# Latent attention of the decode tokens, four sequences at a time in 32-column tiles of TensorE

## The chip, the cores and the metric

The kernel runs on one NeuronCore of a Trainium2 chip, written instruction by instruction with semaphores. The engines are TensorE (PE; its weight loads are listed apart as PEld), VectorE (DVE), ScalarE (ACT), GpSimd (POOL) and SyncE (SP), which issues most DMAs. The metric is the device time of one execution in microseconds. The kernel before took 2738.17, 2734.61 and 2735.32 us in three runs: median 2735.32. TensorE has two clock levels, 1.2 and 2.4 GHz; a granted clock of 1.00 in the profile is the higher one.

## The reference

One layer of a decoder step for 1024 prompt tokens and 8 sampled tokens (8 sequences, one new token each, 2048 cached positions). The change is in the latent attention of the 8 sampled tokens:

```python
def mla_sample(q_nope, q_rope, latent_new, past_latent, w_uk, w_uv):
    scale = (MLA_NOPE_DIM + MLA_ROPE_DIM) ** -0.5          # 64 + 32
    q_abs = jnp.einsum('bthd,chd->bthc', q_nope, w_uk)     # 8 heads, 128 latent dims
    def scores(lat):
        s = (jnp.einsum('bthc,bkc->bhtk', q_abs, lat[..., :MLA_KV_RANK])
             + jnp.einsum('bthr,bkr->bhtk', q_rope, lat[..., MLA_KV_RANK:]))
        return s.astype(jnp.float32) * scale
    ...
    p = jax.nn.softmax(jnp.concatenate([scores(past_latent), s_new], axis=-1), axis=-1)
    o_lat = (jnp.einsum('bhtk,bkc->bthc', p[..., :past_len], past_latent[..., :MLA_KV_RANK])
             + jnp.einsum('bhtk,bkc->bthc', p[..., past_len:], latent_new[..., :MLA_KV_RANK]))
    return jnp.einsum('bthc,chd->bthd', o_lat, w_uv)
```

`past_latent` is gathered from a paged cache: 16 pages of 128 rows for each sequence, 160 values a row (128 latent, 32 rotary). All arrays are fp32.

## The kernel before

The program goes through feed-forward 1, the input projections, the prompt's latent attention (16 steps for each of 4 head pairs), then the **decode latent stage**, then the dilated window attention (prompt and decode together), the merge, and feed-forward 2. The order on each engine is the order of the code; semaphores connect them. Large products are written as three matmuls on fp32r operands: an operand is split into `hi` (rounded) and `lo` (the rest).

The decode latent stage (PE lines 1067 to 1133, ACT 1598 to 1621, DVE 1926 to 1981, POOL 744) works so:

- SP loads the pages of sequence pairs one by one into `latn` (line 563, one issue for each page, with the page number read into a register). The last loads are issued while the stage runs.
- POOL copies the 32 rotary values of each cached row three times side by side into `kr_nat`, 1536 columns for a sequence.
- For each of 32 units (sequence b, four pages) PE transposes 4 pages of latents (L1078) and 4 of rotary values (L1079) into PSUM banks 4 + u%2 and 6 + u%2. ACT copies them to `lt_hi` and `krm` (L1610, L1611), DVE writes the rests `lt_lo` and the middle third of `krm` (L1949, L1951).
- PE then multiplies with `z_hi`, `z_lo`, `z_rope` (L1101 to L1104, four matmuls of 512 columns): zero-padded query blocks, which put the 8 heads of each sequence in their own 8 of 64 rows, so that all eight sequences accumulate in PSUM banks 0 to 3. The transposes of unit u+2 are issued before the scores of unit u.
- One softmax for 64 rows by 2048 columns (DVE maximum L1958, ACT exponential L1613, DVE scale L1970), 16 transposes of the probabilities (L1110), copies by ACT.
- Values (L1121, L1123): for each sequence 1 + 16 plain fp32 matmuls, with 8 columns of probabilities as the weights and 128 latent columns moving. Then transposes, `w_uv` (L1132), and the store into `om_hi`, `om_lo`.

SP waits for `latn_read` before it loads the window caches `kv_d` into the place of the latents; POOL's and DVE's first dilated steps wait for them. In the code before, the last `latn_read` comes with the last value matmul.

Of the kernel before, what the change touches and what calls it, by code (L numbers as in the profile page):

```python
# [20 lines left out]
F32 = mybir.dt.float32  # L21
# [8 lines left out]
P = 128  # L30
# [71 lines left out]
def build(nc, io):  # L102
    with ExitStack() as ctx:
# [13 lines left out]
        seq_mask = sb("seq_mask", [NS * MH, NS])  # L117
# [78 lines left out]
        lt_hi = at(24576, "lt_hi", [P, 4, 512], F32R)  # L196
        lt_lo = at(32768, "lt_lo", [P, 4, 512], F32R)
        krm = at(40960, "krm", [96, 4, 512], F32R)
        kr_nat = at(49152, "kr_nat", [P, 2, NPG, 96])

        z_hi = at(61440, "z_hi", [P, NS * 136], F32R)
        z_lo = at(65792, "z_lo", [P, NS * 136], F32R)
        z_rope = at(70144, "z_rope", [96, NS * 136], F32R)
        wukT = at(74496, "wukT", [64, MH * P])
        wuv = at(78592, "wuv", [P, MH * 64])
        qabs = at(80640, "qabs", [P, NS, MH])
        q_rope = at(80896, "q_rope", [32, NS, MH])
        s_tmp = at(81152, "s_tmp", [NS * MH, NS])
        s_stat = at(81184, "s_stat", [NS * MH, 8])
        s_new = at(81216, "s_new", [NS * MH, NS])  # L210
        s_newT = at(81248, "s_newT", [NS, NS * MH])
        ckv_nat = at(81504, "ckv_nat", [NS, P])
        olat = at(82016, "olat", [P, NS, MH])
        dprobs = at(24576, "dprobs", [NS * MH, PAST])
        dprobsT = at(32768, "dprobsT", [P, NPG, NS * MH])
        olatT = at(36864, "olatT", [MH, NS * P])
# [108 lines left out]
        lt_hi_done = sem("lt_hi_done")  # L325
        lt_lo_done = sem("lt_lo_done")
        lat_read = sem("lat_read")
        latn_read = sem("latn_read")
        q_zeroed = sem("q_zeroed")
        dm_pe = sem("dm_pe")  # L330
        dm_v = sem("dm_v")
        dm_act = sem("dm_act")
# [139 lines left out]
        def pv_ends(S):  # L472
            _, k, kbs = filler(S)
            return k if k is not None and kbs[-1] == 2 * (k % 4) + 1 else None

# [194 lines left out]
        def _(pool):  # L670
# [68 lines left out]
            for b in range(NS):  # L739
                if b % 2 == 0:  # L740
                    pool.wait_ge(latn_landed[b // 2], 16 * 2 * NPG)
                if b >= 2:
                    pool.wait_ge(lt_ready, 4 * (b - 1))
                nc.gpsimd.tensor_tensor(kr_nat[:, b % 2].rearrange("p n (c f) -> p n c f", c=3),
                                        latn[:, latent_slot(b) * NPG:(latent_slot(b) + 1) * NPG, P:LAT].unsqueeze(2).to_broadcast([P, NPG, 3, 32]),
                                        zero[:].unsqueeze(2).unsqueeze(3).to_broadcast([P, NPG, 3, 32]), ALU.add
                                        ).then_inc(kr_packed, 1)
# [15 lines left out]
        def _(pe):  # L763
# [302 lines left out]
            dm = Tally(dm_pe)  # L1066
            def latents_T(u):

                b, k = divmod(u, 4)
                if k == 0 and b % 2 == 0:  # L1070
                    pe.wait_ge(latn_landed[b // 2], 16 * 2 * NPG)
                if k == 0:
                    pe.wait_ge(kr_packed, b + 1)
                if u >= 2:
                    pe.wait_ge(lt_lo_done, 2 * (u - 1))
                for j in range(4):
                    page = 4 * k + j
                    nc.tensor.transpose(ps[:, 4 + u % 2, j * P:(j + 1) * P], latn[:, latent_slot(b) * NPG + page, 0:P], ident[:])  # L1078
                    last = nc.tensor.transpose(ps[0:96, 6 + u % 2, j * P:(j + 1) * P], kr_nat[:, b % 2, page], ident[:])  # L1079
                last.then_inc(lt_ready, 1)  # L1080
# [4 lines left out]

# [6 lines left out]
            pe.wait_ge(dm_v, 4)  # L1092
            pe.wait_ge(dm_act, 4)
            for u in range(4 * NS):
                b, k = divmod(u, 4)
                if u + 2 < 4 * NS:
                    latents_T(u + 2)
                pe.wait_ge(lt_lo_done, 2 * u + 2)
                z = slice(b * P, (b + 1) * P)
                out = ps[:, k, :]  # L1100
# [5 lines left out]
            mm(ps[0:64, 4, 0:NS], qabs[:].rearrange("p b h -> p (b h)"), ckv_s[:], start=True, stop=False)  # L1106
            dm.by(mm(ps[0:64, 4, 0:NS], q_rope[:].rearrange("p b h -> p (b h)"), kr_s[:], start=False, stop=True))
            pe.wait_ge(dm_v, 13)
            for j in range(NPG):
                last = nc.tensor.transpose(ps[:, 5 + j // 8, (j % 8) * 64:(j % 8 + 1) * 64],  # L1110
                                           dprobs[:, j * P:(j + 1) * P], ident[0:64, 0:64])
            dm.by(last)
            nc.tensor.transpose(ps[0:NS, 7, 0:64], s_new[:], ident[0:64, 0:64])
            dm.by(nc.tensor.transpose(ps[0:NS, 7, 64:64 + P], ckv_s[:], ident[:]))
# [1225 lines left out]
```

## Time and profile before

| | |
|---|---|
| median of three runs | 2735.32 us |
| profiled execution | 2738.68 us |
| its span | 2736.6 us, granted clock 0.964 |
| PE busy | 2572.9 us, 94% of the span |
| DVE, ACT, POOL busy | 1100.4, 533.4, 925.0 us |
| decode latent stage, from the last prompt-attention store to the first dilated scores | 1493.9 to 1615.5 us |

A program with PE busy in 94% of its span is bound by PE nearly everywhere, but not in this stage alone: there the busy share, the clock and the engine that ends a wait change from stretch to stretch. The page's totals do not tell this; the table of stretches and the chain of waits below do. A matmul's duration in the profile includes the way through the array, so the pace is read from start to start, or from a merged row of many.

### The profile page before, as it was taken

Reading aid. Unit: us, or ns where it says so; the run is one execution under the profiler, and the core shown is the slowest. Engines: PE = TensorE matmul, PEld = TensorE weight load, DVE = VectorE, ACT = ScalarE, POOL = GpSimd, SP = SyncE. Lnnn points to the kernel's source line nnn. Section 1 sums busy time; section 2 is a strip of 40 time slices with the busy share of each in tenths; the row PEclk is TensorE's granted clock in tenths of the full one; section 3 lists DMA queues with packets and bytes.
Section 4 is the critical chain, followed back from the end, with each engine's and each line's share of the span. In section 5 each row is a group of like instructions: output and inputs, shape, how many; then the busy total and the mean of one; then the engine's idle time right before and its main releaser. Section 6 shows DMA issues by size and latency. Waiting matters only on the chain.

```text
span 2736.6 us, 40136 instructions
## 1 busy us (share of the span) xinstructions
PE 2572.9 (94%) x15962; PEld 2426.5 (89%) x15962; DVE 1100.4 (40%) x1881; ACT 533.4 (19%) x1250; POOL 925.0 (34%) x468
## 2 busy tenths in 40 slices
PE   4999999999989999999888889889899999999996
PEld 4999999999979998998555758789799999999996
DVE  7122222222274663101667624473612222222226
ACT  4100000000022430213334513211310000000002
POOL 5333333333354340531000210234333333333332
PEclk9999999999999999999999987789899999999998
DMA  4121212121222341421202142463112211111111
GB/s 157 68 90 68 90 68 89 68 89 68 89 99 91 136 144 46 142 91 61 66 14 69 58 157 101 139 204 117 41 64 82 95 47 47 47 47 47 47 47 62
DMA packets 85101, 229.38 MB, mean 84 GB/s; under 512 B 8681, under 2 KB 47122, under 8 KB 83826
## 3 DMA queue, kind: packets, MB, share of 16 engines
q1 hardware_dynamic: 78858, 207.86, 22.0%
q10 hardware_dynamic: 6088, 19.23, 1.8%
q8 instruction: 126, 2.06, 0.3%
q14 instruction: 29, 0.24, 0.0%
HBM read 196.65 MB, written 74.39 MB: 99 GB/s over the span
## 4 chain that ended last, share of the span: by engine, by line
PE 51%; DVE 5%; issue 2%; ACT 2%; DMA 2%; POOL 0%; SPq 0%; DVEq 0%; ACTq 0%; POOLq 0%
PE ps L768 13%; PE ps L769 12%; PE ps L770 12%; PE ps L1219 1%; PE ps L1034 1%; PE ps L1016 1%; PE ps L1123 1%; PE ps L881 1%; PE ps L883 1%; PE ps L882 1%; DMA sgt<-scratch_gates 1%; PE ps L1001 1%; PE ps L1184 1%; PE ps L1202 1%; PE ps L1078 1%
## 5 line engine op out<-in xcount | busy, mean ns | idle before, releaser
L768 PE MATMUL ps<-u_hi,w_hi 128*128 128x352 f32 (+1 forms) x2880 | 933.1, 324 | 25.3 <-DVE u_lo L403 18.9
L769 PE MATMUL ps<-u_lo,w_hi 128*128 128x352 f32 (+1 forms) x2880 | 925.2, 321 | 0.0
L770 PE MATMUL ps<-u_hi,w_lo 128*128 128x352 f32 (+1 forms) x2880 | 923.2, 321 | 0.0
L677 POOL TENSOR_TENSOR w_hi<-raw,zero 128x1024 fp32r<-128x1024 f32 x184 | 352.6, 1916 | 1322.3 <-PE ps L768 1108.3
L768 PEld LDWEIGHTS ps<-u_hi,w_hi 128*128 128x128 f32 x2880 | 545.8, 189 | 36.1 <-DVE u_lo L403 17.6
L769 PEld LDWEIGHTS ps<-u_lo,w_hi 128*128 128x128 f32 x2880 | 546.5, 190 | 0.5 <-issue 0.3
L770 PEld LDWEIGHTS ps<-u_hi,w_lo 128*128 128x128 f32 x2880 | 545.6, 189 | 0.0
L680 POOL TENSOR_TENSOR w_lo<-raw,w_hi 128x1024 fp32r<-128x1024 f32 x184 | 450.4, 2448 | 14.4
L1735 DVE TENSOR_TENSOR h<-ps,silu 128x352 f32<-128x352 f32 x132 | 68.2, 516 | 750.6 <-PE ps L770 745.3
L1744 DVE SCALAR_TENSOR_TENSOR x<-ps,x 128x352 f32<-128x352 f32 (+1 forms) x528 | 270.9, 515 | 211.8 <-PE ps L770 211.6
L768 PE MATMUL ps<-h_hi,w_hi 128*128 128x352 f32 (+1 forms) x1056 | 344.0, 326 | 10.0 <-DVE x L1744 7.3
L769 PE MATMUL ps<-h_lo,w_hi 128*128 128x352 f32 (+1 forms) x1056 | 340.9, 323 | 0.0
L770 PE MATMUL ps<-h_hi,w_lo 128*128 128x352 f32 (+1 forms) x1056 | 340.0, 322 | 0.0
L768 PEld LDWEIGHTS ps<-h_hi,w_hi 128*128 128x128 f32 x1056 | 200.5, 190 | 18.7 <-DVE x L1744 18.3
L1387 ACT ACTIVATE silu<-ps 128x352 f32<-128x352 f32 x132 | 60.7, 460 | 757.5 <-PE ps L770 757.5
L769 PEld LDWEIGHTS ps<-h_lo,w_hi 128*128 128x128 f32 x1056 | 200.8, 190 | 0.3
L770 PEld LDWEIGHTS ps<-h_hi,w_lo 128*128 128x128 f32 x1056 | 201.1, 190 | 0.0
L1391 ACT ACTIVATE h_hi<-h 128x352 fp32r<-128x352 f32 x132 | 65.2, 494 | 494.7 <-DVE h L1735 494.7
L1739 DVE TENSOR_TENSOR h_lo<-h,h_hi 128x352 fp32r<-128x352 f32 x132 | 101.8, 771 | 65.0 <-ACT h_hi L1391 65.0
L1436 ACT ACTIVATE swapped<-ps 32x352 f32<-32x352 f32 (+1 forms) x144 | 64.9, 450 | 87.2 <-PE ps L770 74.6
L1320 ACT ACTIVATE sq<-x 128x352 f32<-128x352 f32 (+1 forms) x96 | 45.4, 489 | 158.4 <-DVE x L1744 80.2
L1001 PE MATMUL ps<-kT,qT 128*128 128x512 f32 (+3 forms) x192 | 74.0, 495 | 2.1 <-ACT probs L1545 2.1
(271 smaller groups left out, 2767.0 us busy)
## 6 DMA issues: line engine op xcount, KB each, us to landing
raw<-in_wstream SPq DMA_DIRECT2D x186, 512.0 KB, 3.2
out_win_out<-in_cache_win SPq DMA_DIRECT2D x23, 1424.0 KB
latn<-in_cache_mla SPq DMA_DIRECT2D x128, 80.0 KB, 1.9
scratch_gates<-stage ACTq DMA_DIRECT2D x16, 516.0 KB, 2.6
out_win_out<-in_cache_win SPq DMA_DIRECT2D x7, 1168.0 KB
kv_d<-in_cache_win SPq DMA_DIRECT2D x24, 256.0 KB, 9.0
sgt<-scratch_gates SPq DMA_DIRECT2D x16, 352.0 KB, 4.1
scratch_x_mid<-x SPq DMA_DIRECT2D x1, 4128.0 KB, 13.3
```

The source lines that it names most:

```text
L677: nc.gpsimd.tensor_tensor(hi, raw[:, s % RAW], zero[:].to_broadcast([P, UW]), ALU.add).then_inc(w_hi_done, 1)
L680: nc.gpsimd.tensor_tensor(lo, raw[:, s % RAW], hi.bitcast(F32), ALU.subtract).then_inc(split_done, 1)
L768: a = mm(out, wh, xh, start=start, stop=False)
L769: mm(out, wh, xl, start=False, stop=False)
L770: return a, mm(out, wl, xh, start=False, stop=stop)
L1001: last = mm(ps[:, bank, 0:w], qT[i % 2][h][:, n * P:(n + 1) * P], kT[i % 2][h][:, a * P:a * P + w], start=True, stop=not diag)
L1387: A(silu[:, b, 0:w], ps[:, t, 0:w], ACT.Silu).then_inc(silu_done, 1)
L1391: A(h_hi[:, par, c, tile(t)], h32[:, b, 0:w], ACT.Copy).then_inc(h_hi_done, 1)
L1436: last = A(swapped[a:a + 32, e % 2, 0:w], ps[b:b + 32, bank, 0:w], ACT.Copy)
L1735: V.tensor_tensor(h32[:, b, 0:w], ps[:, 3 + t, 0:w], silu[:, b, 0:w], ALU.mult).then_inc(h_mul, 1)
L1739: V.tensor_tensor(h_lo[:, par, c, tile(t)], h32[:, b, 0:w], h_hi[:, par, c, tile(t)].bitcast(F32), ALU.subtract).then_inc(h_ready, 1)
L1744: V.scalar_tensor_tensor(x[:, m, tile(t)], ps[:, 6 + j % 2, 0:TILES[t][1]], 0.5, x[:, m, tile(t)], ALU.mult, ALU.add).then_inc(down_evac, 1)
```

## The change

- The split of latents and queries is dropped in the scores: plain fp32 matmuls, which the profile records as two instructions each.
- Four sequences form a group; two groups r = 0, 1. In a group, sequence q has the 32 columns 32q to 32q+31 of the array (8 heads used, the rest zero), so its scores fall into PSUM partitions 32q to 32q+31. The weights are `qabs[:, b]` (128 by 32), the moving operand `lt` (128 by 512).
- Rotary part: POOL packs 16 pages by 32 values without repeats; one transpose turns four pages into a 128 by 128 block `krT`; the weights `q_rope[:, i]` hold the query in rows 32i to 32i+31 and zeros elsewhere, so four matmuls of 128 columns do the four pages.
- PSUM units are copied once, by ACT and DVE in turns.
- Each group has its own softmax over 128 rows by 2048 columns. The normalization moves behind the values. PE does the transposes of later units meanwhile.
- Values: four matmuls next to each other with 128 by 32 weights and `latn` moving; `latn_read` is raised by 4 after each group.

```diff
+            def decode_scores(quad):
+                r, k = divmod(quad, 4)
+                pe.wait_ge(lt_act, 4 * quad + 4)
+                pe.wait_ge(lt_dve, 4 * quad + 4)
...
+                if quad == 4:
+                    pe.wait_ge(dm_act, DMA_EXP[0])
+                for q in range(4):
+                    mm(ps[32 * q:32 * q + 32, k, :], qabs[:, 4 * r + q], lt[:, (4 * quad + q) % 8],
+                       start=True, stop=False, skip_group_check=True)
+                for i in range(4):
+                    for q in range(4):
+                        last = mm(ps[32 * q:32 * q + 32, k, i * P:(i + 1) * P], q_rope[:, i, 4 * r + q],
+                                  krT[:, (4 * quad + q) % 8], start=False, stop=i == 3, skip_group_check=True)
+                last.then_inc(dsc_ready, 1)
...
-                mm(out, z_hi[:, z], lt_hi[:, u % 4], start=b == 0, stop=False)
-                mm(out, z_lo[:, z], lt_hi[:, u % 4], start=False, stop=False)
-                mm(out, z_hi[:, z], lt_lo[:, u % 4], start=False, stop=False)
-                mm(out, z_rope[:, z], krm[:, u % 4], start=False, stop=b == NS - 1).then_inc(lat_read, 1)
...
+                            last = mm(ps[rows, bank, 0:P], dprobsT[:, r, j, rows],
+                                      latn[:, latent_slot(4 * r + q) * NPG + j, 0:P], start=False, stop=j == NPG - 1,
+                                      skip_group_check=True)
+                last.then_inc(latn_read, NS // 2)
...
+            for u in range(2, 8):
+                latents_T(u)
...
+            for quad in range(8):
+                decode_scores(quad)
+                if quad < 6:
+                    for q in range(4):
+                        latents_T(4 * (quad + 2) + q)
+            decode_PT(0)
+            decode_values(0)
+            decode_PT(1)
+            decode_values(1)
...
+            def latents_copy(u):
+                act.wait_ge(lt_ready, u + 1)
...
+                if u % 2:
+                    A(lt[:, u % 8], ps[:, 4 + u % 2, :], ACT.Copy).then_inc(lt_act, 1)
+                else:
+                    A(krT[:, u % 8], ps[:, 6 + u % 2, 0:P], ACT.Copy).then_inc(lt_act, 1)
...
+            for u in range(20):
+                latents_copy(u)
+            decode_exp(0)
+            for u in range(20, 32):
+                latents_copy(u)
```

On PE, the end of one unit of the score loop before: the last of four pairs of transposes of unit u+2 (`latn`, `kr_nat`), then the four split matmuls of unit u, which accumulate over all sequences.

```order
L1078 MATMUL ps<-ident,latn_99 128x128
L1079 MATMUL ps<-ident,kr_nat_103 96x128
L1101 MATMUL ps<-lt_hi_100,z_hi_104 128x512
L1102 MATMUL ps<-lt_hi_100,z_lo_105 128x512
L1103 MATMUL ps<-lt_lo_101,z_hi_104 128x512
L1104 MATMUL ps<-krm_102,z_rope_106 128x512
```

The same place now: the end of the new-token scores, the first quad of scores and the transposes of unit 8, which those of units 9 to 11 follow.

```order
L1162 MATMUL ps<-ckv_s,qabs_105 128x8
L1164 MATMUL ps<-kr_s,q_rope_106 128x8
L1099 MATMUL ps<-lt_100,qabs_105 32x512 x4
L1103 MATMUL ps<-krT_101,q_rope_106 32x128 x16
L1082 MATMUL ps<-ident,latn_99 128x128 x4
L1083 MATMUL ps<-ident,kr_nat_103 128x128
```

A quad of scores is 20 matmuls on 32-row outputs, between blocks of four units of transposes (5 each, not 8); the new-token scores moved from behind the loop to ahead of it.

On PE behind the scores, now: `dprobs` are the probabilities, `s_new` and `ckv_s` the new token's.

```order
L1099 MATMUL ps<-lt,qabs 32x512 x4
L1103 MATMUL ps<-krT,q_rope 32x128 x16
L1118 MATMUL ps<-ident,dprobs 128x128 x16
L1124 MATMUL ps<-ident,s_new 8x128
L1126 MATMUL ps<-ident,ckv_s 8x128
L1140 MATMUL ps<-ckv_nat,s_newT 32x128 x4
L1143 MATMUL ps<-latn,dprobsT 32x128 x64
```

This block of transposes and values comes once for each group, where before 16 transposes stood ahead of all eight sequences' values.

On DVE, where the first softmax stands among the copies (the end of unit 19 and the start of unit 20 around it):

```order
L2011 COPY krT<-ps 128x128 [waits dsc_ready,lt_ready]
L2017 TENSOR_REDUCE s_stat<-ps 128x1 [waits dsc_ready]
L2020 TENSOR_TENSOR s_stat<-s_stat 128x1 [waits dm_v]
L2022 TENSOR_SCALAR s_stat<-s_stat 128x1 [waits dm_v]
L2013 COPY lt<-ps 128x512 [waits dsc_ready,lt_ready]
```

The maximum over the first group stands ahead of the copies of unit 20; ACT has its exponential at the same place. In the kernel before no softmax step stood among the copies.

## Rows read from the trace of the kernel before

**Rows 1.** From the page: the span, and the page loads (x, KB, us to landing).
```profile
span 2736.6 us, 40136 instructions
latn<-in_cache_mla SPq DMA_DIRECT2D x128, 80.0 KB, 1.9
```

**Rows 2.** Stretches: us, busy (x) of PE, PEld, DVE, ACT, POOL; clock; DMA; GB/s.
```profile
1493.90:1507.50 13.60, 6.03 (x32) 5.56 (x32) 9.64 (x12) 4.22 (x9) 5.75 (x2) 0.62 0.22 60
1507.50:1568.70 61.20, 60.23 (x372) 48.60 (x372) 42.80 (x64) 32.41 (x60) 16.49 (x6) 0.97 0.18 62
1568.70:1579.30 10.60, 2.86 (x20) 1.99 (x20) 4.79 (x10) 3.33 (x5) 0.00 (x0) 0.51 0.00 0
1579.30:1611.90 32.60, 32.58 (x271) 23.73 (x270) 0.00 (x0) 0.00 (x0) 0.00 (x0) 0.95 0.01 2
```

**Rows 3.** Chain that ended last: start us, us, what.
```profile
1332.86 1.72 PE ps L1001 x4
1493.95 3.10 DVE z_hi L1929
1497.04 3.75 DVE z_lo L1929
1501.41 3.56 PE ps L1089 x16
1568.81 2.21 DVE s_stat L1958
1571.41 2.06 ACT dprobs L1613 x2
1584.89 3.59 PE ps L1123 x32
1613.30 5.64 DMA kv_d<-in_cache_win
```

**Rows 4.** Timeline of the loop: start us, us, engine, line, work [idle before].
```profile
1496.04 0.30 PE L1078 MATMUL ps<-ident,latn 128*128 128x128 f32 x1 [2.97 <-POOL kr_nat L744]
1507.83 0.42 PE L1079 MATMUL ps<-ident,kr_nat 128*96 128x128 f32 x1
1509.11 0.42 PE L1079 MATMUL ps<-ident,kr_nat 128*96 128x128 f32 x1
1511.11 0.27 PE L1079 MATMUL ps<-ident,kr_nat 128*96 128x128 f32 x1
1511.76 0.27 PE L1079 MATMUL ps<-ident,kr_nat 128*96 128x128 f32 x1
1563.93 0.27 PE L1079 MATMUL ps<-ident,kr_nat 128*96 128x128 f32 x1
1564.24 0.60 ACT L1610 ACTIVATE lt_hi<-ps 128x512 fp32r<-128x512 f32 x1 [0.73 <-PE ps L1079]
```

**Rows 5.** Groups, 1489.6 to 1615.6: work xcount, busy us, mean ns, idle before.
```profile
L744 POOL TENSOR_TENSOR kr_nat<-latn,zero 128x1536 f32<-128x1536 f32 x8 | 23.0, 2878 | 151.1 <-PE ps L1034 115.2 <-PE ps L1079 35.9
L1949 DVE TENSOR_TENSOR lt_lo<-ps,lt_hi 128x512 fp32r<-128x512 f32 x32 | 22.1, 692 | 15.8 <-ACT krm L1611 15.7
L1610 ACT ACTIVATE lt_hi<-ps 128x512 fp32r<-128x512 f32 x32 | 19.1, 597 | 28.4 <-PE ps L1079 28.4
```

**Rows 6.** Timeline, column tiles of 64 and a switch of tiling.
```profile
1486.98 0.63 PEld L1034 LDWEIGHTS ps<-probsT,v_pair 128*64 128x64 f32 x8 [0.17 <-issue]
1489.61 3.46 PE L1034 MATMUL ps<-probsT,v_pair 128*64 128x256 f32 x32 [0.73 <-DVE probsT L1896]
1614.16 0.64 PE L1132 MATMUL ps<-olat,wuv 128*64 128x8 f32 x16 [0.32 <-DVE olat L1977]
```

**Rows 7.** Stretches, for the granted clock.
```profile
1511.00:1568.00 57.00, 56.39 (x358) 45.34 (x357) 40.93 (x60) 31.33 (x58) 16.49 (x6) 1.00 0.18 63
1497.30:1507.50 10.20, 4.77 (x23) 4.27 (x20) 6.24 (x10) 3.11 (x8) 2.35 (x1) 0.50 0.23 64
```

**Rows 8.** Timeline, SyncE: the last page loads.
```profile
1482.78 32.79 SPq L563 DMA_DIRECT2D latn<-in_cache_mla  x25
```

More of the change, by code:

```diff
@@ L741, in _ @@
                     pool.wait_ge(latn_landed[b // 2], 16 * 2 * NPG)
[L742 to L746, printed above, removed]
+                nc.gpsimd.tensor_tensor(kr_nat[:, b].rearrange("p (n f) -> p n f", f=32),
+                                        latn[:, latent_slot(b) * NPG:(latent_slot(b) + 1) * NPG, P:LAT],
+                                        zero[:].unsqueeze(2).to_broadcast([P, NPG, 32]), ALU.add
                                         ).then_inc(kr_packed, 1)
@@ L1067, in latents_T @@
             def latents_T(u):
-                b, k = divmod(u, 4)
-                if k == 0 and b % 2 == 0:
+                quad, q = divmod(u, 4)
+                r, k = divmod(quad, 4)
+                b = 4 * r + q
+                if k == 0 and q % 2 == 0:
                     pe.wait_ge(latn_landed[b // 2], 16 * 2 * NPG)
@@ L1074, in latents_T @@
                 if u >= 2:
-                    pe.wait_ge(lt_lo_done, 2 * (u - 1))
+                    pe.wait_ge(lt_act, u - 1)
+                    pe.wait_ge(lt_dve, u - 1)
+                first = latent_slot(b) * NPG + 4 * k
                 for j in range(4):
-                    page = 4 * k + j
-                    nc.tensor.transpose(ps[:, 4 + u % 2, j * P:(j + 1) * P], latn[:, latent_slot(b) * NPG + page, 0:P], ident[:])
-                    last = nc.tensor.transpose(ps[0:96, 6 + u % 2, j * P:(j + 1) * P], kr_nat[:, b % 2, page], ident[:])
@@ L1080, in latents_T @@
-                last.then_inc(lt_ready, 1)
+                    nc.tensor.transpose(ps[:, 4 + u % 2, j * P:(j + 1) * P], latn[:, first + j, 0:P], ident[:])
+                nc.tensor.transpose(ps[:, 6 + u % 2, 0:P], kr_nat[:, b, k * P:(k + 1) * P], ident[:]
+                                    ).then_inc(lt_ready, 1)
+            def decode_scores(quad):
+                r, k = divmod(quad, 4)
+                pe.wait_ge(lt_act, 4 * quad + 4)
+                pe.wait_ge(lt_dve, 4 * quad + 4)
+                if quad == 0:
+                    pe.wait_ge(dm_v, DM_QABS)
+                    pe.wait_ge(dm_act, DMA_ROPE)
+                if quad == 1:
+                    pe.wait_ge(dm_v, DM_SN)
+                if quad == 4:
[8 more added lines that the diff above has]
+                last.then_inc(dsc_ready, 1)
@@ L1106, in _ @@
[L1106 to L1111, printed above, removed]
-            dm.by(last)
@@ new lines, in _ @@
+            dm.by(last)
+            for quad in range(8):
+                decode_scores(quad)
+                if quad < 6:
+                    for q in range(4):
+                        latents_T(4 * (quad + 2) + q)
[3 more added lines that the diff above has]
+            decode_values(1)
+            pe.wait_ge(dm_v, DM_SCALED)
+            for r in range(2):
+                last = nc.tensor.transpose(ps[:, 1, r * P:(r + 1) * P], olat_n[:, r], ident[:])
@@ L1612, in _ @@
[L1612 to L1619 removed]
+            act.wait_ge(q_zeroed, 2)
@@ new lines, in _ @@
+            dve.wait_ge(dm_v, n)
+            n = dv.by(V.tensor_reduce(s_stat[:, :, 0], s_tmp[:], axis=AX, op=ALU.add))
+            assert n == DM_SN
+            dve.wait_ge(dm_v, n)
+            for u in range(8, 20):
+                latents_copy(u)
+            decode_max(0)
+            for u in range(20, 32):
+                latents_copy(u)
+                if u == 23:
+                    decode_den(0)
+            probs_copy(0)
+            decode_max(1)
+            probs_copy(2)
+            new_kept(0)
```

267 lines of the change are left out of this document (154 added, 113 removed).

## The prediction

> **What bounds the kernel now.** I read the page first. The span is 2736.6 us [rows 1], nearly all of it dense TensorE (PE) work that the change does not touch. So I looked for the decode latent stage with the table of stretches [rows 2]: it starts when the last prompt-attention rows are stored (1493.9) and ends at 1615.5, 121.6 us. The chain of waits [rows 3] says what ends last in each stretch.
>
> Preparation, 1493.9 to 1507.5: two zero fills on VectorE (DVE), 3.10 and 3.75 us, then eight small matmuls of 3.56 us; PE is busy 6.0 of 13.6 us. The score loop, 1507.5 to 1568.7: PE is busy 60.2 of 61.2 us, so PE bounds it; without the first transposes that is 59.6 us for 32 units, 1.86 each. Softmax gap, 1568.7 to 1579.3: PE is busy 2.9 of 10.6 us, the chain is DVE's maximum and ScalarE's (ACT) exponential. Values, 1579.3 to 1611.9: PE alone, 3.59 us for each sequence of 16 matmuls (32 records) plus 0.31 for the new token. Then 3.6 us of output steps, while the chain has left through the DMA of the window caches (kv_d), which is issued once the latents have been read: the end of the values, at 1611.9, is what counts for the rest of the program.
>
> **Paces.** A transpose of 128 by 128 starts every (1511.76 - 1511.11)/6 = 0.108 us at full clock, and (1509.11 - 1507.83)/6 = 0.213 us at half [rows 4]. A plain fp32 matmul is two records: 1.72/4 = 0.43 us per record of 512 columns, 3.59/32 = 0.112 per record of 128 [rows 3]; I round to 0.427 and 0.107, which is two cycles per column. Two column tiles of 64 do run side by side: the 28 records of 256 columns and 4 of 128 in line 1034 would need 28 x 0.213 + 4 x 0.107 = 6.4 us one after the other and took 3.46 [rows 6]. At tiny sizes, two tiles start a record every 0.64/16 = 0.040 us or less [rows 6]. No row shows four tiles.
>
> **The change part by part.** PE's plain count in the stage: transposes of latents fall from 256 to 160 (32 units of 4 latent pages and one packed rope block), 27.6 to 17.3 us. The 128 split score matmuls of 512 columns go (four stand in the 1.86 us unit beside 8 transposes: 1.86 - 0.86 = 1.0, 32 us in all). In their place stand 32 fp32 matmuls of 512 columns and 128 of 128; the values keep 128 + 8 matmuls of 128 columns, now 32-wide tiles. In records: 64 x 0.427 + (256 + 272) x 0.107 = 83.8 us if they ran singly, 20.9 us four abreast. I take four abreast: from the 1034 row, whose tiles each keep their own full pace. The lower end is 20.9 us; the upper is 83.8. A near miss, 0.040 per small record as in the tiny row, would add 528 x 0.013 = 7 us.
>
> I now walk the stage. *Preparation.* The fills covered 2176 columns in 6.9 us, 3.2 ns each, beside GpSimd's (POOL's) rope copies [rows 3]. Now 256 + 1024 columns: 4.1 us, 2.8 less. POOL's copy is a third as large (1536 to 512 columns, 2.9 to about 1 us [rows 5]), so the first transposes come earlier, which only fills a wait. The small matmuls then end at 1502.1 instead of 1505.0. But six more units of transposes now stand before the first scores, at half clock as that stretch has 0.50 [rows 7]: 6 x 5 x 0.213 = 6.4 us, then four new-token matmuls with 128-wide weights, 8 records at the 0.22 us of line 1089 (3.56/16): 1.8 us. First scores start at 1510.3; before it was 1509.2. The six units are drawn forward from the loop, not added.
>
> *Loop.* A quad of scores is 8 x 0.427/4 + 32 x 0.107/4 = 1.7 us. The transposes for a quad: two units of 5 x 0.108 = 0.54 go at once; the third needs the bank back. In the loop before, ACT starts 0.31 us after the start of the last transpose (1563.93 to 1564.24) [rows 4]; a copy of 512 columns takes 0.69 on DVE or 0.60 on ACT [rows 5]; so unit three starts 0.43 + 0.31 + 0.69 + 0.06 = 1.49 us after unit one, and the four take 1.49 + 1.07 = 2.56 us. The copies of 128 columns are not in the trace, between nothing and 0.69; I take 0.3, and even at 0.69 the engine's 1.38 per two units stays under 1.49. Going to tiles and back costs time: the first tiled weight load after transposes sat 0.17 us on "issue" [rows 6]; I give 0.2 each way. A quad is then 1.7 + 2.56 + 0.4 = 4.7 us, where four units took 7.4.
>
> A rule speaks against the change here: the Trainium skill, TensorEngine Tiling (Array Packing), Key Properties, says that changing the tiling mode, not just the tile, drains TensorE. The 0.17 us row agrees in kind; the change alternates some 18 times, 3 to 4 us by the row; the rule itself comes without a price.
>
> Quad 0 runs partly at half clock: it ends at 1512.4. Three more quads with transposes end at 1512.4 + 3 x 4.7 = 1526.5. Quad 4 must wait for the first softmax: on DVE and ACT it stands ahead of the copies of units 20 and after. PE issues two units (1.1 us) and stops. Maximum to exponential and its small steps: 4.9 us as before (2.21 from 1568.81, then 2.06 from 1571.41 and a small companion), since time there goes by the 2048 columns and not by the rows [rows 3]; then a copy, two units and the quad: 8.5 us in all, 1535.0. Quads 5 and 6 with transposes and quad 7 without: 1546.2. The stall is some 4 us of an idle PE, and the clock fell to 0.50 in the preparation, where PE had idled 2.97 us [rows 4, 7]. I allow one spell of ten us at half clock, 4.5 us: scores end at 1550.7, 17.3 before the old 1568.0.
>
> *Second half.* Four groups of four transposes, with DVE's second maximum between the first and the second copy; the new-token copies follow it, so values 0 start about 0.4 + 0.3 + 0.7 + 2.7 + 0.7 + 0.5 = 5.3 us after the scores; 17 x 8 records x 0.107/4 = 3.6 us, with start and drain 4.2. The second exponential is hidden behind them. Then transposes and copies of group 1 (2.6), its new-token step (0.9) and values 1 (4.0): the values end 17.0 us after the scores, plus 4 for half clock behind the 2.7 us gap: 1571.7. The old gap and values took 43.9 us. The scale of the probabilities is gone with it.
>
> *Cover.* Quad 4's transposes now want sequences 6 and 7 at about 1522; the last page load is issued at 1515.6 and lands in 1.9 us [rows 1, 8], plus two POOL copies of 1 us: 1519.5. Covered by 2.5 us; without cover, the delay goes one for one. From the end of the values on nothing is changed: kv_d is issued there and the chain goes on through it. The output steps get a little shorter, off the chain.
>
> **Sum.** Preparation +1.1, loop -18.4, the rest -22.9: values end at 1571.7 instead of 1611.9, -40.2 us. The profiled execution took 2738.68 us around its span of 2736.6; it becomes 2698.5. It lies 3.4 above the median 2735.32, so I forecast 2695.
>
> **Rivals.** *Two abreast.* If only two 32-column tiles stream at a time, the tile work is 41.9 instead of 20.9 us: the gain is 40.2 - 20.9 = 19.3, 2716. For it: two is all that any row shows. Against: each of the two has its own weight load and its own full pace in line 1132 and 1034, and nothing in them looks like a shared stream.
> *One after the other, the slower side.* In the score quads and the values, matmuls on 32-column tiles are serial: 83.8 us. PE never idles then, so take the all-warm walk (40.2 + 8.5 = 48.7 gained) less 62.9: 14 slower, 2749. It decides from 83.8/f = 20.9 + 40.2, an overlap f under 1.4. Against it: 1034's pairs, f = 1.85 to 2.
> *Half clock throughout.* PE waits more often now. At 1.2 GHz instead of 2.4 the walk costs again 20.9 for tiles, six times 4.3 - 2.56 for transpose quads and 3.4 for those of the probabilities: 48.7 - 35 = 14 gained, 2721. Against: in the old loop transposes were 0.86 of each 1.86 us and the clock was 1.00 from 1511 to 1568 [rows 7]; now they are 2.1 of 4.7.
> By the Trainium skill, TensorE: Matmul & The Clock Gate, Part 4, transposes do not count as TensorE activity in the same way. That would favour this rival; the trace agrees only so far that the short transposes around the softmax ran at 0.51 [rows 2].
> *Hidden anyway.* The stage would have to be covered by DMA; the old window moves few bytes and PE ends it, so I give this little.
>
> **Chances.** Forecast 0.72 (a gain of 30 to 50: 2685 to 2705); two abreast 0.12; half clock 0.08; serial 0.05; no net effect 0.03. A difference under 0.2%, 5.5 us, is about what a measurement of this kernel cannot tell from none. Faster 0.93, same 0.02, slower 0.05. The low end, 2684, is the all-warm walk (48.7) and 3 us of clock luck later on; the high end takes in two abreast: 2717.
>
> **What would show it.** In the new trace: 4 tiled score matmuls of 512 columns (8 records) within 0.9 us, and 64 value matmuls (128 records) in 3.5 to 4.5 us; a quad every 4.7 us; one PE gap of about 4 us after quad 3, released by ACT; the values' end near 1572. Records of the tiles that start 0.1 us apart at 128 columns would prove the serial rival; 0.05 the two-abreast one. A wait of quad 4's transposes on latn or kr_nat would show the cover gone. Wrong all round would be a stage after 1615.5 that gets longer by more than 3 us.

## The result, and the profile after

The changed kernel took 2689.82 us, the median of four runs (2688.68 to 2693.64), beside 2735.39 (2734.61 to 2738.17) for the kernel before: a ratio of 0.9833, 95% interval 0.9817 to 0.9848, 45.6 us less. The forecast was 2695. The profiled execution took 2693.64 us. Its page begins so, where [rows 1] had 2736.6:

```profile
span 2691.6 us, 40337 instructions
```

The table of stretches is cut at five events: the starts of the last prompt value record, of the first and the last score record, and of the first and the last value record. Columns as in [rows 2].

```profile
1491.70:1508.20 16.50, 12.49 (x70) 11.38 (x66) 8.85 (x14) 5.01 (x13) 7.19 (x6) 0.69 0.23 62
1508.20:1545.30 37.10, 31.41 (x438) 22.20 (x440) 13.99 (x32) 12.51 (x27) 2.04 (x2) 0.95 0.29 100
1545.30:1550.90 5.60, 3.00 (x42) 2.06 (x34) 4.18 (x7) 2.58 (x3) 0.00 (x0) 1.00 0.00 0
1550.90:1563.20 12.30, 11.33 (x283) 10.33 (x281) 2.28 (x7) 2.05 (x5) 0.00 (x0) 0.86 0.02 4
```

I call the first row the preparation, the second the loop, the last two together the rest, and all of it the stage. Cut at the same events, the kernel before had 16.4, 58.4 and 44.0 us, a stage of 118.8; now it is 71.5, which is 47.3 less. What comes ahead of it was 1.1 us shorter in this execution, and what follows the values 3.4 us longer: 47.3 + 1.1 - 3.4 = 45.0, the difference of the two spans.

The chain of waits in the stage (start us, us, what), to be read against [rows 3]:

```profile
1493.38 1.98 DVE q_rope L1999
1496.35 1.00 DVE qs_all L2004
1497.48 3.55 PE ps L1154 x16
...
1508.27 0.99 PE ps L1099 x8
1509.27 0.87 PE ps L1103 x32
1510.93 0.70 DVE lt L2013
...
1513.05 0.99 PE ps L1099 x8
...
1524.43 2.30 DVE s_stat L2017
1527.34 1.67 issue
1529.38 0.17 ACT krT L1663
...
1531.24 1.87 PE ps L1099 x8
...
1550.94 5.30 PE ps L1143 x128
...
1559.85 3.67 PE ps L1143 x128
```

Eight records of 512 columns pass in 0.99 us, where one took 0.43 [rows 3], and 32 records of 128 columns in 0.87. The second quad comes 4.78 us behind the first, the next two every 4.72 us. In each, one piece of DVE stands on the chain: the copy at 1510.93, for which the third unit's transposes wait. The two groups' values take 5.30 us (in part at half clock, see below) and 3.67 us for 128 records each; before, 32 records took 3.59 [rows 3]. The timeline of PE shows the two waits of the loop, for the bank and behind quad 3 (in brackets the idle time before, and what ended it):

```profile
1511.77 0.63 PE L1082 MATMUL ps<-ident,latn 128*128 128x128 f32 x4 [0.38 <-DVE lt L2013]
...
1529.60 0.66 PE L1082 MATMUL ps<-ident,latn 128*128 128x128 f32 x4 [3.99 <-ACT krT L1663]
```

The stretches cut where the granted clock changes (the column behind POOL's):

```profile
1496.30:1506.50 10.20, 9.02 (x42) 8.67 (x43) 4.12 (x9) 3.75 (x10) 2.95 (x3) 0.50 0.21 57
1506.50:1530.40 23.90, 18.87 (x251) 14.23 (x250) 9.98 (x21) 9.02 (x19) 2.04 (x2) 1.00 0.48 161
1530.40:1533.80 3.40, 3.40 (x33) 1.69 (x35) 1.34 (x5) 0.88 (x2) 0.00 (x0) 0.51 0.00 0
...
1550.90:1554.30 3.40, 3.40 (x72) 3.29 (x72) 0.46 (x3) 0.85 (x3) 0.00 (x0) 0.50 0.03 5
```

Behind the preparation there are two spells at 1.2 GHz, each 3.4 us long, and each begins just behind an idle stretch of PE: 0.8 us after the end of the 3.99 us, and 0.4 us after the end of 2.25 us (the wait for `ckv_nat`, until 1550.52). PE was busy through both, so by estimate they cost the work that the higher clock would have done beside it: 1.7 us each.

### The profile page after: what moved, and what is told of

It is laid out like the page before. It is cut to its first block, busy times and chain, and to the rows that moved or that the text cites. A ratio compares the mean times of both kernels' runs of the same rounds, so it can differ in the third digit from the quotient of the medians.

```text
span 2691.6 us, 40337 instructions
## 1 busy us (share of the span) xinstructions
PE 2526.8 (94%) x16073; PEld 2389.7 (89%) x16073; DVE 1073.7 (40%) x1857; ACT 513.6 (19%) x1222; POOL 911.4 (34%) x468
## 4 chain that ended last, share of the span: by engine, by line
PE 51%; DVE 6%; issue 3%; ACT 2%; DMA 2%; POOL 0%; SPq 0%; DVEq 0%; ACTq 0%; POOLq 0%
PE ps L768 13%; PE ps L769 13%; PE ps L770 12%; PE ps L1270 2%; PE ps L1034 1%; PE ps L1016 1%; PE ps L881 1%; PE ps L883 1%; PE ps L882 1%; DMA sgt<-scratch_gates 1%; PE ps L1001 1%; PE ps L1235 1%; PE ps L1215 1%; PE ps L1253 1%; PE ps L1082 1%
## 5 line engine op out<-in xcount | busy, mean ns | idle before, releaser
L768 PEld LDWEIGHTS ps<-u_hi,w_hi 128*128 128x128 f32 x2880 | 545.6, 189 | 38.2 <-DVE u_lo L401 17.9
L768 PEld LDWEIGHTS ps<-h_hi,w_hi 128*128 128x128 f32 x1056 | 198.9, 188 | 21.1 <-DVE x L1813 20.5
L1487 ACT ACTIVATE swapped<-ps 32x352 f32<-32x352 f32 (+1 forms) x144 | 64.6, 449 | 87.4 <-PE ps L770 78.9
```

The lines of the kernel that those rows point to most:

```text
L768: a = mm(out, wh, xh, start=start, stop=False)
L1487: last = A(swapped[a:a + 32, e % 2, 0:w], ps[b:b + 32, bank, 0:w], ACT.Copy)
```

## The experiments

Each is one edit to the changed kernel. The stage columns are from the profiled execution of each, cut at the same events; where the code is the same, single executions agree in loop and rest to about 0.1 us unless a spell at half clock falls otherwise, and in the preparation to 0.4 us. Every set had the kernel before beside it (medians 2736.14, 2733.73 and 2735.84 us for the second to fourth set); it moved by up to 2.4 us between sets, so differences of medians below are good to about that, except within set 4.

| kernel | set | us (lowest to highest) | ratio, 95% | preparation | loop | rest | stage |
|---|---|---|---|---|---|---|---|
| before | 1 | 2735.39 (2734.61 to 2738.17) | 1 | 16.4 | 58.4 | 44.0 | 118.8 |
| changed | 1 | 2689.82 (2688.68 to 2693.64) | 0.9833, 0.9817 to 0.9848 | 16.5 | 37.1 | 17.9 | 71.5 |
| vals_serial | 2 | 2710.94 (2708.34 to 2716.76) | 0.9905, 0.9889 to 0.9922 | 16.4 | 37.1 | 41.4 | 94.9 |
| vals_pairs | 2 | 2696.53 (2692.75 to 2698.37) | 0.9853, 0.9837 to 0.9870 | 16.7 | 37.1 | 25.8 | 79.5 |
| scores_serial | 2 | 2720.16 (2713.96 to 2723.28) | 0.9935, 0.9918 to 0.9951 | 16.7 | 69.4 | 16.2 | 102.4 |
| warm | 2 | 2688.36 (2685.77 to 2693.43) | 0.9831, 0.9815 to 0.9848 | 16.5 | 35.5 | 16.2 | 68.2 |
| exp_later | 3 | 2684.59 (2682.45 to 2688.81) | 0.9820, 0.9804 to 0.9837 | 16.7 | 34.2 | 17.8 | 68.7 |
| banks3 | 3 | 2686.27 (2681.22 to 2690.57) | 0.9819, 0.9800 to 0.9838 | 16.7 | 33.2 | 17.9 | 67.8 |
| prep | 3 | 2687.72 (2684.59 to 2690.36) | 0.9831, 0.9815 to 0.9847 | 14.4 | 36.9 | 19.2 | 70.6 |
| combined | 3 | 2684.20 (2675.84 to 2688.36) | 0.9809, 0.9788 to 0.9829 | 13.0 | 35.5 | 16.7 | 65.1 |
| after_again | 4 | 2688.66 (2686.25 to 2691.05) | 0.9828, 0.9815 to 0.9842 | 16.5 | 37.1 | 17.9 | 71.5 |
| combined_again | 4 | 2683.75 (2681.96 to 2685.47) | 0.9809, 0.9795 to 0.9822 | 13.3 | 33.6 | 18.1 | 65.0 |
| cover | 4 | 2685.48 (2685.05 to 2688.61) | 0.9818, 0.9805 to 0.9832 | 13.0 | 33.2 | 18.1 | 64.3 |
| comb_warm | 4 | 2682.34 (2679.97 to 2683.54) | 0.9804, 0.9791 to 0.9818 | 13.2 | 35.2 | 16.2 | 64.6 |

**vals_serial: the values tile by tile.**

```diff
-                for j in range(-1, NPG):
-                    for q in range(4):
+                for q in range(4):
+                    for j in range(-1, NPG):
```

> The changed kernel, but in the values all 17 matmuls of one sequence are issued before those of the next (column tile by column tile) instead of the four tiles in turn. Same instructions, same data. Theory (the gain of the values is four column tiles streaming at once, and needs them to alternate in the queue): 2 x 68 matmuls at 0.213 us one after the other, 14.5 us per group instead of 3.7 to 5.3; the values' end moves by about 20 us and the kernel takes about 2710. Rival (the gain is only the shorter weight load, 32 columns, or TensorE looks far enough ahead to overlap the tiles in any order): the stage keeps its length, 2690.

The instructions are the same, in another order, and the chain shows one sequence after the other:

```profile
1562.44 3.61 PE ps L1143 x32
1566.05 0.33 PE ps L1140 x2
```

32 records take 3.61 us, what they took before the change [rows 3], and the two behind them are the next sequence's new token. So the four 32-column tiles by themselves give nothing: the matmuls overlap only when neighbours in PE's queue are of different tiles. The rest grew by 23.5 us and the median by 21.1, as expected.

**vals_pairs: tiles 0 and 1, then 2 and 3.**

```diff
-                for j in range(-1, NPG):
-                    for q in range(4):
+                for j, q in [(j, q) for pair in (0, 2) for j in range(-1, NPG) for q in (pair, pair + 1)]:
```

> The changed kernel with the values of column tiles 0 and 1 in turn first, then those of tiles 2 and 3 in turn. Theory (as many tiles stream as alternate): two abreast, 7.3 us per group at full clock instead of 3.7, +7 us in all, about 2697. Rival (overlap independent of the order): 2690.

```profile
1555.14 3.62 PE ps L1143 x64
```

One, two and four tiles in turns pass 32, 64 and 128 records in 3.61, 3.62 and 3.67 us: each tile keeps its full pace, and four times 3.61 us of work pass in 3.67.

**scores_serial: each sequence's five score matmuls together.**

```diff
                 for q in range(4):
                     mm(ps[32 * q:32 * q + 32, k, :], qabs[:, 4 * r + q], lt[:, (4 * quad + q) % 8],
                        start=True, stop=False, skip_group_check=True)
-                for i in range(4):
-                    for q in range(4):
+                    for i in range(4):
```

> The changed kernel, but each score quad goes sequence by sequence: the 512-column matmul of a tile and its four rotary ones, then the next tile. Theory: a quad's 1.86 us becomes up to 6.8 (4 x 0.853 + 16 x 0.213); seven quads have their copies hidden behind it, which gives back about 0.8 us each, so the loop grows by some 33 to 39 us, to about 2725: the whole gain of the loop (22 us) and more is the tiles' overlap. If TensorE looks a few matmuls ahead, it is less: five matmuls per tile could overlap at the seams only. Rival (the gain comes from dropping the split and its copies): well under 2710.

Its chain, through one quad (every L1099 record is one of 512 columns, 0.427 us alone):

```profile
1516.26 0.97 PE ps L1099 x2
1517.23 0.55 PE ps L1102 x5
1517.78 0.11 PE ps L1099
...
1521.21 0.88 PE ps L1102 x8
1522.08 0.59 PE ps L1082 x4
```

The quad's scores last from 1516.26 to 1522.08, 5.82 us where the changed kernel has 0.99 + 0.87: 3.96 more, 31.7 for eight, and the loop grew by 32.3. At the seams the next tile's first record starts among the last one's, which is all of the overlap that is left. That is less than the 33 to 39 us expected: the seams gave more, but no copy came to be hidden behind the scores, since from one quad to the next it is 8.68 us instead of 4.72, again 3.96 more. The two serial orders together would cost 55.8 us (an estimate: they were not run together), more than the 47.3 us that the stage gained. So without the overlap of the tiles the change would have been a loss.

**warm: dummy matmuls in PE's two idle stretches.** Seven plain fp32 matmuls of 256 columns ahead of unit 20's transposes, five behind the first group's transposed probabilities, into banks that nobody reads then.

```diff
+                    if quad == 3:
+                        pe.wait_ge(lt_act, 20)
+                        pe.wait_ge(lt_dve, 20)
+                        for _ in range(7):
+                            mm(ps[:, 4, 0:256], ident[:], rope_m[:, 0:256], start=True, stop=True)
...
             decode_PT(0)
+            for _ in range(5):
+                mm(ps[:, 6, 0:256], ident[:], rope_m[:, 0:256], start=True, stop=True)
```

> The changed kernel with 7 extra fp32 matmuls of 256 columns (0.43 us each) ahead of unit 20's transposes, inside the 4 us softmax stall, and 5 ahead of the first values, inside the 2.2 us wait; their results are overwritten. Theory (my prediction charged 8.5 us for half clock behind these stalls, the trace shows two spells of 3.4 us): with the stalls filled the two spells go, quad 4 takes 1.9 instead of 3.2 us and values 0 3.7 instead of 5.3, so the values end 2 to 3 us sooner, 2687. Rival (the extra matmuls delay something, or the spells only move into the later stages): 2690 or above.

```profile
1508.40:1543.90 35.50, 32.87 (x455) 24.19 (x454) 13.97 (x32) 12.52 (x27) 2.04 (x2) 1.00 0.31 104
1549.40:1560.10 10.70, 9.73 (x283) 8.80 (x281) 2.28 (x7) 2.12 (x5) 0.00 (x0) 1.00 0.01 3
```

Both stretches now stand at 1.00, and the stage is 3.3 us shorter: that is the price of half clock in loop and rest, less what the dummies themselves may cost. The median moved by 1.5 us, less than the runs scatter. The rival, that the spells only move, is not ruled out for the program as a whole: this trace has one of 3.4 us just behind the stage, from 1564.75 on.

**exp_later: the first exponential behind ACT's copies of units 20 and 21.**

```diff
-            for u in range(20):
+            for u in range(22):
                 latents_copy(u)
             decode_exp(0)
-            for u in range(20, 32):
+            for u in range(22, 32):
```

> One edit to the changed kernel: ACT's first exponential goes behind its copies of units 20 and 21, not ahead of them. In the changed kernel PE stood idle 3.99 us, until ACT's copy of unit 20's rope block at 1529.6, which stands behind the exponential; DVE's copy of the same unit was ready to go after its maximum. Theory (the order of ACT's queue, not the softmax itself, ends that wait): PE starts unit 22 when DVE's copies are there, about 1.8 us earlier, and quad 4, which needs the exponential at 1529.4, starts then instead of at 1531.2: the score loop 37.1 -> about 35.3 us, the stage 71.5 -> 69.7, total 2687 to 2689. Rival (the exponential is on the path whatever its place: moved back it delays dm_act, and quad 4 starts as late as before): loop 37.1 or up to 0.6 longer, total as the changed kernel.

```profile
1527.74 0.63 PE L1082 MATMUL ps<-ident,latn 128*128 128x128 f32 x4 [2.26 <-DVE lt L2013]
...
1529.40 1.07 PE L1099 MATMUL ps<-lt,qabs 128*32 128x512 f32 x8 [0.38 <-DVE krT L2011]
```

The wait of 3.99 us became 2.26 and 0.38, quad 4 runs in 1.07 us and no spell at half clock follows: loop -2.9, of which about 1.3 is the shorter wait and 1.6 the clock, as in warm. ACT's order did stand on the path. Quad 4 waits for the exponential by the code, and by the trace too: its second step ended at 1529.25, 0.14 us ahead of quad 4 as in banks3 and combined; the copy that the view names is of a later unit. The 1.6 us cannot be counted on: banks3, combined and cover below have the same 5.16 us from the end of quad 3 to the start of quad 4 and did meet a spell there, combined_again did not.

**banks3: three banks for the latents, the rotary blocks of a quad in one.** Unit u goes to bank 4 + u%3; four rotary transposes go to bank 7 and are copied once.

```diff
-                if u >= 2:
-                    pe.wait_ge(lt_act, u - 1)
-                    pe.wait_ge(lt_dve, u - 1)
+                if u >= 3:
+                    pe.wait_ge(lt_act if (u - 3) % 2 else lt_dve, (u - 3) // 2 + 1)
...
+                if q == 3:
+                    if quad >= 1:
+                        pe.wait_ge(kr_copied, quad)
+                    for j in range(4):
+                        last = nc.tensor.transpose(ps[:, 7, j * P:(j + 1) * P], kr_nat[:, 4 * r + j, k * P:(k + 1) * P], ident[:])
+                    last.then_inc(kr_ready, 1)
```

> One edit to the changed kernel: the transposed latents go through three PSUM banks in turns instead of two, and the rotary blocks of a quad through one bank, transposed together and copied once (512 columns). The changed kernel's quads come every 4.72 us: 0.99 + 0.87 us of scores and some 2.8 us for four units of transposes, of which 20 transposes of 0.108 us are 2.16. Theory (what is left over is the wait for a bank to come back): the wait for a bank goes, a quad comes every 4.0 to 4.1 us, loop 37.1 -> 32 to 33 us, total 2684 to 2686. Rival (the period is set by the rate of the copies, two engines at 0.6 to 0.8 us for each 512 columns: four of latents and one of rope on two engines are 3.2 to 3.6 us per 2 quads per engine, or by the switch of tilings): period stays at 4.6 to 4.7 us and the total at 2689.

```profile
1513.84 0.99 PE ps L1106 x8
...
1515.71 2.03 PE ps L1081 x16
1517.74 0.44 PE ps L1089 x4
1518.18 1.00 PE ps L1106 x8
```

The chain of the loop is PE alone, and a quad comes every 4.34 us, not 4.0: 16 transposes take 2.03 where 16 x 0.108 would be 1.73. The loop lost 3.9 us: 0.4 for each of the five quads that come regularly, 1.6 behind quad 3 and 0.3 from the clock. So of the 4.72 us some 0.4 was a wait for a bank that a third bank removes. By the starts of single records a quad still hesitates 0.13 us ahead of its fourth unit, and the changes of tiling cost 0.1 us towards the tiles (203 ns to the next start instead of 109) and 0.17 back; the rest, some 3.9, is work. The 4.0 expected had left these out.

**prep: DVE sums the queries ahead of its two zero fills.**

```diff
+            V.tensor_copy(samp[64:96, 0:MH], qs_all[96:128]).then_inc(qs_kept, 1)
+            dve.wait_ge(qs_kept, 9)
+            V.tensor_tensor(qs_all[64:96], qs_all[64:96], samp[64:96, 0:MH], ALU.add).then_inc(qs_kept, 1)
             V.tensor_tensor(qabs[:].rearrange("p b h -> p (b h)"), zero[:].to_broadcast([P, NS * 32]),
...
-            V.tensor_copy(samp[64:96, 0:MH], qs_all[96:128]).then_inc(qs_kept, 1)
-            dve.wait_ge(qs_kept, 9)
-            V.tensor_tensor(qs_all[64:96], qs_all[64:96], samp[64:96, 0:MH], ALU.add).then_inc(qs_kept, 1)
```

> One edit to the changed kernel: DVE makes the summed queries (a copy and an add on 32 rows, 0.93 and 1.00 us in the changed kernel, 0.19 and 0.22 before) ahead of its two zero fills instead of behind them. They do not need the fills; the wukT product on PE needs only them and started at 1497.5. Theory (the fills stand on the path to wukT, and through its eight matmuls and their copy on the path to the first scores): wukT starts at 1494.0 to 1495.5, preparation 16.5 -> 14 us, total 2687 to 2688. Rival (six units of transposes at half clock or POOL's rope packing set the first scores): preparation stays within 0.5 us of 16.5. Beside it: if the two small operations are slow because POOL's packing starts at 1492.06, they take about 0.2 us when they run ahead of that and about 0.9 where they run beside it.

The timeline: PE's `wukT` product, ACT's steps, and the first transposes behind them (of the four rows, PE's last waits for ACT's second):

```profile
1491.89 2.09 PE L1154 MATMUL ps<-qs_all,wukT 64*128 64x8 f32 x16
...
1494.52 1.31 ACT L1654 ACTIVATE q_rope<-qs_all 32x64 f32<-32x64 f32 x4 [5.07 <-DVE q_rope L2002]
...
1495.85 0.28 ACT L1663 ACTIVATE krT<-ps 128x128 f32<-128x128 f32 x1
...
1496.38 1.09 PE L1082 MATMUL ps<-ident,latn 128*128 128x128 f32 x4 [2.40 <-POOL kr_nat L744]
```

The `wukT` product starts 3.1 us behind the last prompt values, not 5.8, but the preparation fell by 2.1 only: PE idles 2.40 us again ahead of unit 2. The view names POOL, whose last packing ends just then, but unit 2 needs only the third of six; by the code it needs ACT's copy of unit 0 (1495.85), and PE's queue got past the wait for it at 1496.17, 0.04 us behind the end of that copy. The copy stands behind `q_rope` (1494.52), and that waits for the fill that now comes last. So the fills are on the path still, in another way, and the gain is smaller than the 2.5 us expected. The two small steps did not come ahead of POOL's packing: the copy began 0.2 us before the end of a packing step (1489.93, 1490.15) and took 0.26 us, the sum began just behind the start of the next and took 0.99. In this execution the rest is 1.3 us longer, with a spell of 6.8 us at half clock.

**combined and combined_again: the three edits together.**

> The three edits together (three latent banks with one rope bank, the exponential two units later, the query sums ahead of the fills). Theory (three different waits on one path, so the gains add): -2.6 - 5 - 1.8 = about 9 us, stage 71.5 -> 62 to 63, total about 2680 to 2682. Rival (a common resource, the copies of ACT and DVE or the window loads, catches up with PE): less than 6 us, 2684 or more.

> The three edits together once more, beside the changed kernel on one chip. By the stages of the traces (71.5 us against 65.1) it should be 6 us below the changed kernel; by the medians of the last two sets it was 2 to 4 below. Expected 4 to 7 us below. Rival (the stage's gain is given back in the later part): within 2 us.

The stage fell by 6.4 and 6.5 us, not 9. Beside the changed kernel in one set the median is 4.9 us lower, and the two ranges do not touch. PE's timeline of combined shows where the missing time is:

```profile
1516.39 1.09 PE L1081 MATMUL ps<-ident,latn 128*128 128x128 f32 x8 [0.28 <-DMA latn<-in_cache_mla]
1518.51 0.66 PE L1089 MATMUL ps<-ident,kr_nat 128*128 128x128 f32 x4 [1.02 <-POOL kr_nat L746]
...
1524.45 0.66 PE L1081 MATMUL ps<-ident,latn 128*128 128x128 f32 x4 [1.95 <-DVE lt L2022]
...
1526.19 1.58 PE L1106 MATMUL ps<-lt,qabs 128*32 128x512 f32 x8 [0.66 <-ACT s_stat L1679]
```

The last page loads and their packing, covered by some microseconds before, now end last. And two of the gains were one: banks3 alone already starts quad 4 as soon as the exponential is there (its own quad 3 ended at 1524.42 and quad 4 started at 1529.54, after maximum and exponential), so exp_later had nothing left to give. On the other side the preparation fell by 3.5 and 3.2 us, more than the 2.1 of prep alone; the code offers a reason, not tested by itself: with three banks unit 2 no longer waits for ACT's copy of unit 0.

**cover: the same, with the scores of sequences 6 and 7 made from the latents of sequences 4 and 5**, which have long landed. It leaves out the true scores of two sequences, so it only prices the wait.

> The three edits together, with one part of the data changed: the scores of sequences 6 and 7 are made from the latents of sequences 4 and 5, which have long landed, so PE does not wait in the score loop for the last page loads and their rope packing (it waits for them before the last quad instead). With the three edits PE stood 0.28 us on the last page load and 1.02 us on POOL's packing, around 1516 to 1518. Theory (the cover of those loads is used up by the faster loop, and what is left over from the expected 9 us is 1.5 us of this, 1 us of the bank wait and the overlap of two edits in one wait): quad 3 ends 1.3 to 1.6 us earlier behind the first quad, loop 35.5 -> 34, total 1.5 us below the three edits. Rival (the loads are covered, the time goes elsewhere): loop 35 to 36.

```profile
1518.52 0.60 PE L1090 MATMUL ps<-ident,kr_nat 128*128 128x128 f32 x4
...
1526.15 1.94 PE L1110 MATMUL ps<-lt,qabs 128*32 128x512 f32 x8
```

Both waits are gone, the rotary transposes of quad 4 at 1518.52 follow without one: from the first scores to the start of the transposes behind quad 3 there are now 14.9 us (1505.99 to 1520.92) where combined_again had 16.3 (1504.02 to 1520.35). That 1.4 us is inside the 1.3 to 1.6 expected. Its loop fell by 0.4 only against combined_again, since here a spell at half clock met quad 4 (1.94 us for its first eight records), and the median does not show it: 2685.48 against 2683.75, where 1.5 us less had been expected.

**comb_warm: combined with dummy matmuls**, six ahead of unit 20's transposes and five ahead of the first values.

> The three edits together, and dummy matmuls on PE in its two idle stretches (six and five plain fp32 matmuls of 256 columns, into a bank that nobody reads). With the three edits PE ran at half clock from 1526.6 for 3.4 us, right behind the idle 1.95 us of the first softmax, and quad 4 took 3.3 us where others take 1.9. Theory (the half clock is what is left of the loop's loss): quads 4 in 1.9 us, loop 35.5 -> 34 us, second stretch up to 1.6 us shorter, total 2 to 3 us below the three edits. Rival (dummies stand in the way of the transposes as much as they give): within 1 us.

The loop has a clock of 1.00 throughout and is no shorter for it. ACT's timeline tells why:

```profile
1522.10 0.60 ACT L1676 ACTIVATE lt<-ps 128x512 f32<-128x512 f32 x1 [4.93 <-PE ps L1081]
1522.72 1.97 ACT L1683 ACTIVATE dprobs<-ps,s_stat 128x2048 f32<-128x2048 f32 x1
```

The exponential stands behind unit 21's copy, whose transposes now stand behind the dummies: 4.3 us from the end of quad 3 to its start, against 2.8 in combined_again. That 1.5 us is about as much as the spell at half clock had cost combined (3.4 us long, so 1.7 by estimate). Behind the loop the rest is 0.5 and 1.8 us shorter than in the two runs of combined. This is the fastest version measured, 6.3 us under the changed kernel in the same set with ranges that do not touch, and 1.4 us under combined_again, which is less than either scatters.

**after_again: the changed kernel once more.**

> The changed kernel itself once more, so that the next three stand beside it on one chip. Its profiled execution of before had a last part (from the end of the values on) of 1128.4 us, and nine traces of kernels that are alike in that part gave 1122.5 to 1128.4. Theory (that part differs only by the phases of the granted clock, so the 3.4 us that it lost against the kernel before are luck of one execution): stage 71 to 72 us again, last part anywhere in 1122 to 1129. Rival (the change costs something there, as the window loads now start at another time): 1128 or more again.

```profile
1564.30:2686.60 1122.30, 1055.44 (x6616) 1022.03 (x6608) 446.22 (x770) 171.25 (x469) 392.07 (x194) 0.95 0.25 85
```

The stage came out as 71.5 us again and the part behind the values as 1122.3, where the first trace had 1128.4 at a clock of 0.94. Over the thirteen traces of the changed kernel and its variants, alike in that part, it lies between 1122.3 and 1128.4, and the kernel before stands between with 1125.0. So the 3.4 us were a matter of one execution.

## Why the prediction was right, and where it was off

*Four abreast* was right, and its three rivals of mechanism fell. Serial: vals_serial brings back 3.61 us per 32 records and scores_serial 5.82 us for a quad, the changed kernel's order does not. Two abreast: vals_pairs is that case, at 7.9 us more for the values alone. *Half clock throughout*: the loop stood at 1.00 from 1506.5 to 1530.4, with 20 x 0.108 = 2.2 of each 4.72 us in transposes. *Hidden anyway* fell with the 45.6 us themselves.

*A quad every 4.7 us*: 4.72. Its parts held as well: scores 1.7 predicted, 0.99 + 0.87 measured. A quad that follows another without transposes between takes 0.86 for the first eight records, so going to tiles costs 0.13 us and, by the starts of single records, going back 0.17, where I had given 0.2 each. The four units of transposes took 2.7 us, not 2.56, so small errors cancel in the 4.72. By the Trainium skill, TensorEngine Tiling (Array Packing), Key Properties, a change of tiling mode drains TensorE; the trace agrees so far that each change costs time, 0.3 us for the pair; a drain itself it does not show.

*The stall behind quad 3*, about 4 us: 3.99, ended by ACT, as said. exp_later, with 2.26 and 0.38, shows that 2.6 of them were softmax, the rest ACT's order.

*Preparation +1.1*: it was +0.1. The two fills took 0.53 and 1.98 us on the chain, not 4.1; the sum of the queries behind them took 0.93 and 1.00 instead of 0.19 and 0.22 and gave that back (last section). The gain of 1.0 against the forecast lies behind them: six units of transposes and the new-token matmuls took 7.2 us (1501.03 to 1508.27), not 8.2; the clock was back at 1.00 from 1506.5 on, and I had taken all of it at half.

*Loop -18.4 and the rest -22.9*: -21.3 and -26.1. The step that failed is the allowance for half clock, 4.5 us in the loop for "one spell of ten us" and 4 in the rest. The spells were 3.4 us each and warm measures their price: 1.6 and 1.7 us, 3.3 together instead of 8.5. I had taken the length of the spell from the preparation, where PE's idle time went on into it; in the loop PE was back at dense work before it began. That this made it short is not shown: in the loop of scores_serial a spell that began 1.1 us ahead of PE's return lasted 6.8 us, but in prep one that began 0.3 us ahead of it lasted 3.4. Without allowances my walk gave 35.9 for the loop and 17.0 for the rest; warm has 35.5 and 16.2. The mechanism was right and one term of 8.5 was 5.2 too large, with 1.0 from the preparation and 1.2 from small steps: 7.4, against 7.1 us between -40.2 and -47.3.

*Cover*, 2.5 us: POOL's last packing ends at 1519.00 and unit 19, which needs it, starts at 1521.79, a margin of 2.8; with a loop that comes 4.6 us sooner to these units the loads ended last (combined). On POOL:

```profile
1516.96 2.04 POOL L744 TENSOR_TENSOR kr_nat<-latn,zero 128x512 f32<-128x512 f32 x2 [17.71 <-DMA latn<-in_cache_mla]
```

*Nothing changes behind the values*: right, by after_again; but one pair of executions alone would have told 3.4 us of a loss that is not there, just over my bound of 3 us.

## What to carry to other kernels

Column tiles multiply the pace only if neighbouring matmuls in the queue belong to different tiles; write the loop over tiles innermost. When an engine waits behind a softmax, look at what stands behind the long step on the other engine's queue before looking at the step itself. And gains on one path add only as far as each has a wait of its own: two of three here shared one, and all together ran into the page loads.

## What the runs showed of the hardware

*Small VectorE steps beside GpSimd.* POOL's packing and DVE's steps in the changed kernel's preparation, from its timeline:

```profile
1493.30 2.06 DVE L1999 TENSOR_TENSOR q_rope<-zero 128x1024 f32<-128x1024 f32 x1
1495.39 0.92 DVE L2002 COPY samp<-qs_all 32x64 f32<-32x64 f32 x1
1496.35 0.99 DVE L2004 TENSOR_TENSOR qs_all<-qs_all,samp 32x64 f32<-32x64 f32 x1
...
1494.24 2.02 POOL L744 TENSOR_TENSOR kr_nat<-latn,zero 128x512 f32<-128x512 f32 x1
1496.22 1.03 POOL L744 TENSOR_TENSOR kr_nat<-latn,zero 128x512 f32<-128x512 f32 x1
```

POOL's copy takes 1.03 us, but 2.02 where DVE's fill of 2.06 us lies over its start; it ends at 1496.26, and DVE's copy of 64 columns, begun at 1495.39, ends at 1496.31. The next pair ends at 1497.25 and 1497.34. In the kernel before, the same two DVE steps ran with POOL idle and took 0.19 and 0.22 us. So the two engines did not slow each other in proportion, one waited for the other's instruction to end. The Trainium skill, SBUF — State Buffer, SBUF: two separate sides, says that the two share a port pair, held for a whole instruction as an exclusive lock; the trace agrees to 0.1 us.

The fills show it best when they are counted from the end of the POOL copy that they overlap. In the kernel before, the two POOL copies ended at 1495.90 and 1499.65 and the two fills of 1088 columns at 1497.04 and 1500.80: 1.15 us behind, both times. In the changed kernel the fill of 1024 columns ended 1.08 us behind a copy (1494.28 to 1495.36). That is 1.05 ns per column each time. My 3.2 ns per column was this and the wait for POOL in one figure. The preparation's chain is therefore in part a chain of turns between DVE and POOL, which the prediction had as two separate costs.

*Tiles start nearly together.* In the trace's records the four tiles' matmuls of one step start 6.7 ns apart, and the next four 0.109 us after the first of them: the pace of one tile's 128-column record.
